# A two-block transformer kernel: silu in one function, chunks outermost in 256-token blocks, squares taken early

## What is computed

```python
h = h + sigmoid(h @ w_ple_gate) * (p @ w_ple_proj)      # "ple", the end of block one
h = rmsnorm(h, g_final)
hl = modulate(rms_norm(h, norm1_g[0]), mod_l[0], mod_l[1])   # start of block two
# conv_module(hl), conv_module(hc):
u = hl @ w_pw1; a, gate = split(u); u = a * sigmoid(gate)
u = depthwise_conv(u, 31 taps) + b_dw
u = silu(layer_norm(u, ln_g, ln_b))                     # the layer norm of the title
return u @ w_pw2
```

## Time and profile before

| | us |
|---|---|
| three runs | 1502.19, 1502.89, 1502.93 (median 1502.89) |
| the profiled execution | 1501.14 |
| its span, first to last instruction | 1499.3 |
| PE busy | 1447.8 (97%) |
| PE weight loads busy | 1254.2 (84%) |
| DVE busy | 953.7 (64%) |
| ACT busy | 612.8 (41%) |
| POOL busy | 394.0 (26%) |

### The profile page before, as it was taken

How to read it: one execution, slowest core, us unless ns; L and a number is a source line. 1 busy time by engine, 2 the same in 40 slices (tenths; PEclk the granted TensorE clock), 3 DMA queues, 4 the chain that set the end, 5 groups by cost and what they waited for, 6 DMA issues and landing times.

```text
span 1499.3 us, 24812 instructions
## 1 busy us (share of the span) xinstructions
PE 1447.8 (97%) x10690; PEld 1254.2 (84%) x10690; DVE 953.7 (64%) x1132; ACT 612.8 (41%) x729; POOL 394.0 (26%) x302
## 2 busy tenths in 40 slices
PE   6899999999999999999999999999999999999999
PEld 5898899989999997665677888888887966899999
DVE  6889764566768576767738777255415578586433
ACT  5624455343434464533633222323223457434443
POOL 4985713000004300000002433432320010044553
PEclk9999999999999999999999999999999999999999
DMA  7542334556766556862535564344423400475542
GB/s 249 169 144 88 111 119 141 181 179 211 232 230 222 184 200 206 214 182 77 176 123 203 184 197 138 126 154 141 135 89 113 169 30 1 141 225 175 191 172 81
DMA packets 156084, 236.16 MB, mean 158 GB/s; under 512 B 6576, under 2 KB 126416, under 8 KB 155856
## 3 DMA queue, kind: packets, MB, share of 16 engines
q1 hardware_dynamic: 152336, 230.78, 47.0%
q10 hardware_dynamic: 3648, 3.92, 1.0%
HBM read 227.55 MB, written 1.05 MB: 152 GB/s over the span
## 4 chain that ended last, share of the span: by engine, by line
PE 83%; DVE 11%; ACT 4%; issue 2%; DMA 0%; ACTq 0%; SPq 0%; DVEq 0%
PE bank L2120 25%; PE bank L2121 24%; PE bank L2122 24%; DVE wlo L1160 2%; PE bank L2447 2%; PE bank L2184 1%; DVE stat L1855 1%; DVE alo L1627 1%; ACT whi L686 1%; DVE A L1649 1%; PE bank L2622 1%; PE bank L614 1%; PE bank L2309 1%; PE bank L595 1%; DVE A L1864 1%
## 5 line engine op out<-in xcount | busy, mean ns | idle before, releaser
L2120 PE MATMUL bank<-ahi,whi 128*128 128x256 f32 (+1 forms) x2480 | 790.1, 319 | 16.7 <-POOL alo L630 4.4
L2121 PE MATMUL bank<-alo,whi 128*128 128x256 f32 (+1 forms) x2480 | 780.0, 315 | 0.0
L2122 PE MATMUL bank<-ahi,wlo 128*128 128x256 f32 (+1 forms) x2480 | 779.7, 314 | 0.0
L1160 DVE TENSOR_TENSOR wlo<-raw,whi 128x2048 fp32r<-128x2048 f32 x160 | 367.0, 2294 | 355.7 <-ACT whi L686 355.4
L686 ACT ACTIVATE whi<-raw 128x2048 fp32r<-128x2048 f32 x160 | 306.3, 1914 | 657.2 <-PE bank L2122 657.2
L2120 PEld LDWEIGHTS bank<-ahi,whi 128*128 128x128 f32 x2480 | 474.2, 191 | 66.3 <-issue 19.6
L2122 PEld LDWEIGHTS bank<-ahi,wlo 128*128 128x128 f32 x2480 | 474.3, 191 | 28.7
L2121 PEld LDWEIGHTS bank<-alo,whi 128*128 128x128 f32 x2480 | 474.5, 191 | 26.8 <-issue 0.2
L2083 POOL TENSOR_TENSOR A<-A 128x512 f32 (+1 forms) x48 | 106.8, 2237 | 478.4 <-ACT A L1026 478.4
L2065 POOL TENSOR_TENSOR alo<-A,ahi 128x512 fp32r<-128x512 f32 (+1 forms) x43 | 126.5, 2944 | 351.8 <-ACT ahi L892 351.8
L1521 DVE SCALAR_TENSOR_TENSOR A<-modraw,scc,A 128x1024 f32<-128x1024 f32 x70 | 121.3, 1773 | 0.6
(11 more groups left out here) (308 smaller groups left out, 1238.2 us busy)
## 6 DMA issues: line engine op xcount, KB each, us to landing
raw<-in_w_ff SPq DMA_DIRECT2D x64, 1024.0 KB, 5.3
modraw<-in_w_mod SPq DMA_DIRECT2D x72, 512.0 KB, 4.4
raw<-in_w_in SPq DMA_DIRECT2D x28, 1024.0 KB, 5.1
A<-in_w_mod SPq DMA_DIRECT2D x24, 512.0 KB, 5.6
raw<-in_pw SPq DMA_DIRECT2D x12, 1024.0 KB, 6.6
raw<-in_w_ffn_gate SPq DMA_DIRECT2D x11, 1024.0 KB, 5.5
raw<-in_w_ffn_up SPq DMA_DIRECT2D x11, 1024.0 KB, 5.4
raw<-in_w_ffn_down SPq DMA_DIRECT2D x11, 1024.0 KB, 4.9
```

The costliest lines, as they stand in the source:

```text
L1160: dve.tensor_tensor(wlo[:, k % 2, :], raw[:, (k + 2) % 4, :], whi[:, k % 2, :].bitcast(F32), ALU.subtract).then_inc(wlo_ready, 1)
L2120: pe.matmul(out_, w_hi, a_hi, start=start, stop=False, **kw)
L2121: pe.matmul(out_, w_hi, a_lo, start=False, stop=False, **kw)
L2122: return pe.matmul(out_, w_lo, a_hi, start=False, stop=stop, **kw)
```

## The change

- Layer norm's gate. ACT takes `Silu` with gain and bias in place, in one function; the sigmoid, the identity and DVE's product go, and `lny_ready` with them. ACT's order becomes: silu u, cast u-1. DVE's order becomes: multiply u, low part u-1.
- `feature_block` has the chunks outermost also with 256 tokens, wherever there is a `chunk_wait`. Both m then accumulate in halves of one bank, so only the first matmul of the bank carries the start flag.
- ple: the squares of X are taken one by one within the blocks' loop (`early_squares`), the Sqrt table is loaded after the last; DVE's split of the first pw1 block (`ahead` of l = 3) is cut in two halves, one after the context's reciprocal and one after the last weighted squares, and l = 4 has no split of its own as before; PE's sums of three pairs come before `mod_pieces(16, 4)`, the fourth after; the four `keep_busy` ahead of the spread of the context's roots go and two come after the sums.
- `keep_busy(pb[7], 4)` is added after block 13 of "in", before `ssm_turn(2)`; the second `keep_busy` of `wait_mix` has one matmul in place of four.

```diff
+            def early_squares(u):
+                act.wait_ge(evac["ple"], u + 1)
+                act.activation(ring(SQ_AT[2], u), unit(X, 2, u), ACT.Square).then_inc(sq_ready, 1)
+
             for l in range(5):
...
+                if l >= 2:
+                    early_squares(l - 2)
...
-            squares(act, 2, lambda u: [(evac["ple"], u + 1)])
+            early_squares(3)
+            act.activation(stat[:, 42:43], epsb, ACT.Sqrt)
...
                     act.wait_ge(lnx_ready, u + 1)
-                    if u >= 4:
-                        act.wait_ge(lny_ready, u - 3)
-                    act.activation(csq[:, u % 4, :], cu, ACT.Sigmoid, scale=C["lng"][:, u:u + 1],
-                                   bias=C["lnb"][:, u:u + 1])
-                    act.activation(cu, cu, ACT.Identity, scale=C["lng"][:, u:u + 1], bias=C["lnb"][:, u:u + 1])\
+                    act.activation(cu, cu, ACT.Silu, scale=C["lng"][:, u:u + 1], bias=C["lnb"][:, u:u + 1])\
                        .then_inc(lns_ready, 1)
                 if u >= 1:
                     v = u - 1
-                    act.wait_ge(lny_ready, v + 1)
+                    act.wait_ge(lns_ready, v + 1)
...
+            def late_split(part):
+
+                p = Pos(FIRST["ple"] + 3, 3)
+                x = slice(1024 * part, 1024 * part + 1024)
+                if part == 0:
+                    dve.wait_ge(whi_ready, p.b + 3)
+                m = dve.tensor_tensor(wlo[:, p.k % 2, x], raw[:, (p.k + 2) % 4, x], whi[:, p.k % 2, x].bitcast(F32),
+                                      ALU.subtract)
+                if part == 1:
+                    m.then_inc(wlo_ready, 1)
...
-                but_last("ple")(p)
+                if l < 3:
+                    ahead(p)
+                if l == 4:
+                    late_split(1)
                 if l == 3:
                     dve.wait_ge(ctx_std, 1)
                     dve.reciprocal(rstd[:, 256:320], rstd[:, 256:320]).then_inc(ctx_rstd, 1)
+                    late_split(0)
...
-            for u in range(KD + 2):
+            for u in range(KD + 1):
                 if u < KD:
                     cu = cacc[:, u, :, :].rearrange("p s t -> p (s t)")
                     dve.tensor_tensor(cu, cu, pb[2][:, :], ALU.mult).then_inc(lnx_ready, 1)
-                if 1 <= u <= KD:
+                if u >= 1:
                     v = u - 1
-                    cv = cacc[:, v, :, :].rearrange("p s t -> p (s t)")
-                    dve.wait_ge(lns_ready, v + 1)
-                    dve.tensor_tensor(cv, cv, csq[:, v % 4, :], ALU.mult).then_inc(lny_ready, 1)
-                if u >= 2:
-                    v = u - 2
                     dve.wait_ge(lnhi_ready, v + 1)
...
-                for c, m in ([(c, m) for c in range(kn) for m in ms] if (chunk_wait or free) and t == 512 else
+                shared = chunk_wait is not None and t == T1
+                for c, m in ([(c, m) for c in range(kn) for m in ms] if chunk_wait or free else
                              [(c, m) for m in ms for c in range(kn)]):
...
-                               c == 0, c == kn - 1)
+                               c == 0 and not (shared and m), c == kn - 1, skip_group_check=shared)
...
+                if l == 13:
+                    keep_busy(pb[7], 4)
...
-                    keep_busy(pb[2], 4 if c == 0 else 4)
+                    keep_busy(pb[2], 4 if c == 0 else 1)
...
             pe.wait_ge(evac["ple"], 2)
-            keep_busy(pb[5], 4)
             pe.wait_ge(ctx_rstd, 1)
             spread_quads(pe, pb[2][:, 256:512], rstd[:, 256:320], 64).then_inc(ctx_spread, 1)
-            sums(pe, 2)
-            for u in range(4):
+            def final_sums(u):
+                pe.wait_ge(sq_ready, SQBASE[2] + u + 1)
+                quad_sums(pe, pb[0][:, 0:64], flat(SQ_AT[2], u), 64, u == 0, u == 3).then_inc(sq_used, 1)
                 pe.wait_ge(fin_sq, u + 1)
...
+            for u in range(3):
+                final_sums(u)
             mod_pieces(16, 4)
+            final_sums(3)
+            keep_busy(pb[5], 2)
```

## The result

The changed kernel takes 1505.83 us (median of 14 runs, 1503.96 to 1507.36); the kernel before, run beside it, 1502.21 (14 runs, 1500.23 to 1502.93). The ratio is 1.0025, with a 95% interval of 1.0018 to 1.0032: slower by 3.6 us, where the forecast was 1.8 us faster. The profiled execution took 1506.12 (span 1504.3) against 1501.14 (span 1499.3), so the two traces hold a difference of 5.0 to explain.

A forecast was written before the change was run, and what follows sets the result against it. PE's fixed list of work was taken as the bound, with gains only where PE waits or runs at the low clock. 3.2 - 0.8 - 3.0 - 1.2 = -1.8 us, against 1502.89 giving 1501.1; 8-in-10 range 1498.6 to 1504.8.

The forecast's parts named there:

- The clock after block 13: Block 14 of "in": four keep_busy fill PE's 2.22 idle and keep the clock up, -0.8 us.
- What was kept of it, 0.8: Block 14: of about 1.4 gained, 0.8 stays, since PE's rotation must wait for DVE's, ending at 141.23.
- The gate: Layer norm's gate: ACT and DVE take turns in a closed chain, 2.72 us a chunk against 1.94, +3.2 us.
- Rival 2: Gate's loop not held by its order; PE's 1.39 a chunk sets it: total -9.7, 1493.2; chance 0.07.
- Rival 4: Everything but the gate reaches its upper bound and the gate's turn is 2.6: -3.6, 1499.3; chance 0.07.
- Rival 1: The clock falls in the gate's loop: price 4.5, total +2.7, 1505.6; chance 0.12.
- Chunks outermost: 256-token blocks of out, ffn, ff1b: the second m fills waits for late chunks, gaining 0.3, 1.2, 1.5; -3.0 us.
- Rival 3: Chunks outermost gives nothing, through two m in one bank or late splits: +1.2, 1504.1; chance 0.08.
- The end of ple: End of ple: sums and reciprocal finish earlier, so PE spreads at 564.9 instead of 566.12, -1.2 us; bounds 0.3 to 1.4.

The follow-up runs named there:

- experiment 2: The kernel before with only the four keep_busy matmuls after block 13 added: 1506.53 us, 1.0037 of before.
- experiment 1: The changed kernel without the four keep_busy matmuls after block 13: 1500.48 us, 0.9994 of before.
- experiment 3: The changed kernel with DVE one multiply further ahead in the gate (low part u-2 behind multiply u): 1496.07 us, 0.9968 of before.
- experiment 6: The changed kernel without the keep_busy after block 13 and with cast u-1 ahead of silu u on ACT: 1492.27 us, 0.9942 of before.
- experiment 7: The kernel before with only chunks outermost in 256-token blocks and three keep_busy gone from the mix: 1499.91 us, 0.9989 of before.
- experiment 4: The changed kernel with three more keep_busy matmuls after block 14: 1500.04 us, 0.9993 of before.
- experiment 5: The changed kernel without the keep_busy after block 13 and with DVE one multiply further ahead in the gate: 1493.04 us, 0.9944 of before.
- experiment 9: The changed kernel with cast u-1 ahead of silu u on ACT and three more keep_busy after block 14: 1492.75 us, 0.9941 of before.
- experiment 11: The kernel before with only the end of ple as in the change: 1500.50 us, 0.9991 of before.
- experiment 8: The changed kernel without the keep_busy after block 13 and with the gate as it was before: 1497.55 us, 0.9974 of before.

## Why the forecast was wrong, point by point

- **The clock after block 13, -0.8: the step that failed.** Its bounds were "0 if the clock falls anyway, 0.8 if not". I read the stretch up to PE's rotation and stopped there. The row that I used to cap the gain, DVE's rotation ending at 141.23, was also the row of a new wait: block 14 ends early and PE idles 1.51. By its own numbers (1.4 gained, 0.8 kept) that wait was to be 0.6. The forecast priced it as lost gain and not as an idle of PE behind which the clock could fall once more. Measured: +4.8 alone (experiment 2), and +4.9 in the change (experiment 1). The bounds were 1.6 and -0.8 at worst and best; the true worst case was a stretch of some 10 us at half clock, in work that nothing else bounds.
- **What was kept of it, 0.8: nothing.** "DVE's list there does not move" was wrong. In experiment 1, whose code in this stretch is that of before, DVE's split behind the rotation starts at 142.04 where it was 141.16; PE, and DVE ahead of this list, are late by 0.13 there. So the slack of 0.86 that PE's 142.09 seemed to hide was for the most part this one execution's.
- **The gate, +3.2: right**, +3.04. The turn of 2.72 was 2.70, silu cost what the sigmoid did (0.82 against 0.81; the sentence of the Trainium skill, page "ScalarE: Activation LUTs", that throughput does not depend on the function agrees, and stands there under "Step-by-step: what each stage is for"), and both ways of opening the chain gave its time back (experiments 3 and 6). Rivals 2 and 4, which need a shorter turn, fall with the same rows. (Rival 4's terms, with the links 0.03 shorter, add up to -3.2 and not -3.6; nothing hung on it.)
- **Rival 1, the clock falls in the gate's loop: did not happen.** PE idles 1.00 to 1.04 us before six of the chunks, not the 1.3 that I had, and the granted clock stays at 1.00 from 726 to 754. The Trainium skill, page "TensorE: Matmul & The Clock Gate", section "A second HAM failure mode: psum-queue depth-cycling", warns of frequent short idles; this loop does not show it. This rival's price, 1505.6, is close to the measured 1505.83 by coincidence: the low stretches lay elsewhere. I weighed the clock at the one place where it held and not at the other two.
- **Chunks outermost, -3.0: right in the trace**, -0.3, -1.35, -1.5 (3.1). Out's second block waits for its split, as forecast, and ff1b's starts at 1320.42, when its split has just ended (from 1318.08 on, at the earlier trace rows' 2.28). ffn's is filled (5.82 for 5.96). Rival 3 falls. As medians of a kernel with this part alone only 1.6 show (experiment 7).
- **The end of ple, -1.2: right in its steps**, but -1.5 lies past its bound of 1.4. The last sum ended 4.6 after ple's last matmul (4.7 forecast), a group unblocked took 0.23 (0.22), and the spread stood at 5.95 (6.2), since the steps from the last sum to the spread took 1.3 and not 1.5.
- **What the sum left out: the fall in pw1, +1.6.** I had let a shift pass through untouched stages unchanged. But whether the clock falls behind a wait of 1.2 to 2.3 us differs from execution to execution. Whether a shift in time makes a fall likelier was not tested.

## What to carry to other kernels

Before filling an idle of PE, read what the filled time uncovers: if another engine's row caps the gain, PE will idle in front of that row, and the clock can fall behind that idle too. A low clock in a stretch that another engine bounds is free; moved into PE's own work it costs up to half of its length. When an operation is taken out of a loop over two engines, follow one chunk around both queues: where the last link returns to the first, one more chunk of lead on DVE, or one swap of two operations on ACT, was worth 8 us here where the shorter work had cost 3.

## What the runs showed of the hardware

- How long the clock stayed low differs. In the changed kernel and in experiment 2 it was some 10 us, with thin matmuls (128x64) first behind the idle. With dense matmuls behind the idles of 2.22 and 2.33 it was 3.4 us in most profiles (before: 0.57 in 134 to 138), but 6.8 us in that of experiment 7 (134 to 142 above, and 0.88 in 130 to 134). Whether the thin work is what made it 10 was not tried.
- One and the same wait lowers the clock in one execution and not in the next: 2.33 us in pw1 did in the profiles of the changed kernel and of experiments 4, 5, 7, 9 and 11, not in those of before and of experiments 1, 2, 3, 6 and 8. The 2.22 behind block 13 did in those of before and of experiments 1, 5, 6, 7 and 8, and not in that of 11. The 1.51 behind block 14 did in those of the changed kernel and of experiment 2, and not in those of experiments 3 and 11, whose clock had both been low 70 us earlier (0.66 and 0.65 in 70 to 74). The Trainium skill, page "TensorE: Matmul & The Clock Gate", section "What's actually happening", says that the clock gate's observation runs freely and does not start with the kernel; these executions agree with that. The scatter of these kernels goes with it, some 1.5 us for each 3.4 us at the low clock in PE's own work.
- The same run of DVE operations (from the start of the second L1311, L1314 in experiment 1, to that of the split behind the rotation) took 5.46 us in the profile of before, 135.70 to 141.16, and 6.00 in experiment 1, 136.04 to 142.04, with the same code and with POOL at work beside them in another alignment. It was 6.0 in nine more profiles, and 5.61 and 5.69 in those of experiments 5 and 7. That POOL is the cause was not tested.
